# Attention with a projection woven in: a unit's value products move ahead of the dense pieces

## The chip, the cores and the metric

One NeuronCore of a Trainium2 chip runs the whole step in one launch. The metric is the device time of that core in microseconds; lower is better. Engines are named as the profile does: PE (TensorE matmul), PEld (TensorE weight load), DVE (VectorE), ACT (ScalarE), POOL (GpSimd), SP (SyncE).

## What is computed

One layer of a decoder on 1024 prompt rows and 8 sample rows: input projection, two kinds of heads, output projection, a mixture of experts, a gated embedding. The change is in the stage that computes the prompt's attention heads and, woven into them, the output projection and the router's logits. Cut to what matters there:

```
z = q @ k.T * SB_SCALE + bias                 # 8 heads of 64, strictly causal
log_beta, log_keep = log_sigmoid(z), where(mask, log_sigmoid(-z), 0)
later = cumsum(log_keep, reverse=True) - log_keep      # over the keys
a = where(mask, exp(log_beta + later), 0)
attn = a @ v
h = h + concat(attn, pool) @ w_out
m = rmsnorm(h, g_ffn)
logits = m @ [w_router_group | w_router_expert]
```

## The kernel before

The rows are cut into nine tiles of 128: tile 0 holds the 8 samples, tiles 1 to 8 the prompt. An earlier stage left qT, kT, v_sb and the pooling half of the mixed rows (mixp) in SBUF. The stage of the change begins in the trace at 296.9 us and ends at about 600 us.

**Units.** `units` lists (t, hp, g): a tile t of queries, a pair of heads hp (four of them), and a group g of up to four key blocks of 128, the last group first. Tiles 1 to 4 have one group and so four units each, with 1 to 4 key blocks; tiles 5 to 8 have two groups and eight units each. One unit n goes through these steps:

- `scores` (lines 804 to 817): PE multiplies queries by keys into `p_sc`, two heads beside each other, and adds the causal mask if the unit has the diagonal block. ACT takes two sigmoids of each head (lines 890 and 891), DVE a running product over the keys (`keep`, line 930) and the product `beta` (line 935), which are the attention weights.
- `turn` (lines 818 to 825): PE transposes `beta` into `p_at`. ACT copies it to `aT` (line 898, the semaphore `at_copied`).
- `values` (lines 826 to 837): PE waits for that copy of the same unit, `at_copied` at `turns_to["turn", n] + 1`, and multiplies it by `v_sb` into `p_o`. On the last unit of a tile, `attn` copies `p_o` to `mixT` (ACT, line 904).

The scores run three units ahead: in its turn n, PE transposes unit n, then computes the scores of unit n + 3.

**The projection.** `jobs_in` and `shares` lay the output projection of earlier tiles over the units, as pieces (j, k). k = 1 to 4 are **dense** pieces, each four matmuls of 128x128 weights by 512 columns (line 860; the trace has two records for each). k = 5 is `rows`: PE transposes the 1024 columns of h times g_ffn (line 873), ACT copies them to `hT` (line 910) and squares h (line 913). k = 6 are the router's **logits** (line 867): eight small products of `hT` by 36 columns. A tile of four units, and each half of tile 5, has the dense pieces 1 and 2 in its first unit, 3 and 4 in its second, rows in the third, logits in the fourth. Tiles 6 to 8 have one dense piece in each of their first four units, none in the fifth, rows in the sixth, logits in the seventh, none in the eighth. So 22 units are **dense units**, 8 are **rows units** and 8 are **logit units**. The tail, behind the last unit, does the ninth job by itself. DVE adds the residual to a finished half (line 949, it waits for `w_done`), multiplies it by g_ffn (line 951) and copies the logits (line 954). All jobs but the ninth share one PSUM bank, `p_w`: PE waits for `w_copied` before it fills it again.

**The order.** Every engine is a queue in program order. `plan`, `act_plan` and `dve_plan` (lines 741 to 754) are the lists that PE, ACT and DVE go through. In a unit n, ACT does: the copy of the turn; the rows; the sigmoids of unit n + 3; the attn copy. DVE does: the logits' copy; running products and beta of unit n + 3; the adds of the dense pieces. `fills` and `turns_to` are numbered from `plan`; POOL stores h and m for each `rows` in it. A stage ends in a barrier of all engines.

Of the kernel before, what the change touches and what calls it, by code (L numbers as in the profile page):

```python
# [72 lines left out]
def build(nc, A, O):  # L73
# [19 lines left out]
    with ctx:  # L93
# [635 lines left out]
        def pieces_in(n):  # L729

            of_tile = [q for q in range(len(units)) if units[q][0] == units[n][0]]
            mine = jobs_in.get(units[n][0], [])
            if not mine:
                return []
            per_job = len(of_tile) // len(mine)
            at = n - of_tile[0]
            return [(mine[at // per_job], k) for k in shares[per_job][at % per_job]]
# [3 lines left out]
        plan, act_plan, dve_plan = [[("scores", n) for n in range(3)] for _ in range(3)]  # L741
        for n in range(len(units)):
            t, hp, g = units[n]
            pieces = pieces_in(n)
            scores = [("scores", n + 3)] if n + 3 < len(units) else []
            rows = [("rows", j) for j, k in pieces if k == 5]
            dense = [("piece", (j, k)) for j, k in pieces if k < 5]
            logit = [("piece", (j, k)) for j, k in pieces if k == 6]
            end = [("values", n)] + ([("attn", t)] if n + 1 == len(units) or units[n + 1][0] != t else [])
            plan += [("turn", n)] + scores + rows + dense + logit + end  # L750
            act_plan += [("turn", n)] + rows + scores + dense + logit + end
            dve_plan += logit + scores + dense + end
        tail = [("piece", (T_ALL - 1, k)) for k in range(1, 5)] + [("rows", T_ALL - 1), ("piece", (T_ALL - 1, 6))]
        plan, act_plan, dve_plan = plan + tail, act_plan + tail, dve_plan + tail
# [1180 lines left out]
```

How the kernel before makes its waits and increments, by code:

```python
    def __call__(self, ins):  # L48
        self.n += 1
        ins.then_inc(self.sem, 1)
        self.eng.wait_ge(self.sem, self.base + self.n)
# [178 lines left out]
                def load_burst(n):  # L230
                    jj, bq = BURSTS[n]
                    if n == 0:
                        sp.wait_ge(s_const, 16 * N_CONST)
                    pages = [page_of("cache_kT", 4 * bq + g, 2 * jj + h) for g in range(4) for h in range(2)]
                    if n == 0:
                        sp.wait_ge(wlo_ready, KD)
                    else:
                        sp.wait_ge(scored, n)
                    for g in range(4):
                        for h in range(2):
                            page = pages[2 * g + h]
                            sp.dma_start(v_sb[:, 2 * g + h, :], A["cache_kT"][bass.ds(page, 1), :, :].rearrange("a p n -> (a p) n")).then_inc(s_kp, 16)
# [1 line left out]
                def load_quad(n):  # L244
                    j, bq = QUADS[n]
                    pages = [page_of("cache_v", 4 * bq + g, j) for g in range(4)]
                    if n < 2:
                        sp.wait_ge(wlo_ready, 2 * KD)
                    else:
                        sp.wait_ge(quad_done, n - 1)
                    for g in range(4):
                        page = pages[g]
                        slot = w_raw[(n % 2) * 2 + g // 2][:, (g % 2) * AW:(g % 2 + 1) * AW]
                        sp.dma_start(slot, A["cache_v"][bass.ds(page, 1), :, :].rearrange("a p n -> (a p) n")).then_inc(s_vp[n % 2], 16)
```

## Time and profile before

| | |
|---|---|
| time of the kernel, median of 3 runs | 1416.88 us (1414.88 to 1417.63) |
| the profiled execution | 1417.37 us |
| its span in the trace | 1415.5 us |
| PE busy over the span | 1301.7 us (92%) |
| DVE busy | 880.0 us (62%) |
| ACT busy | 772.2 us (55%) |
| mean granted clock of TensorE | 0.952 |

Times in rows are us from the start of the span. A row of a timeline gives start, duration, engine, line, operation, output and inputs, shapes, and how many instructions were merged (x8); in brackets stands how long the engine had stood idle before it, and for what. A granted clock of 1.00 is 2.4 GHz, 0.50 is 1.2 GHz.

### The profile page before, as it was taken

The numbers are of one execution on the slowest core, as the hardware profiler recorded it, in microseconds if no ns is written. First come the engines' busy times: TensorE is split into PE (matmuls) and PEld (weight loads), VectorE is DVE, ScalarE is ACT, GpSimd is POOL, SyncE is SP. The second block draws the span as 40 slices with busy tenths as digits, with TensorE's granted clock in tenths as the row PEclk, the third lists the DMA queues.
The fourth block names the chain that finished last, engine by engine and source line by source line (L and its number), as shares of the span: only waits on it lengthen the run. The fifth ranks groups of instructions, "written<-read, shape, count | busy, mean of one in ns | idle before, by whom it ended". The sixth has DMA issues, their size and how long they took to land. (4 is left out here: it accounts for less than half of the span.)

```text
span 1415.5 us, 18630 instructions
## 1 busy us (share of the span) xinstructions
PE 1301.7 (92%) x6716; PEld 968.1 (68%) x6716; DVE 880.0 (62%) x851; ACT 772.2 (55%) x888; POOL 214.0 (15%) x227
## 2 busy tenths in 40 slices
PE   7999899999999999717999999999999999939998
PEld 4776666755555666515788787878878788727886
DVE  5535311134535667276888888888888888735543
ACT  5435311144444656204777777777777777734452
POOL 3000100000000000023222222222222222100000
PEclk9999899979999999956999999999999999959999
DMA  8766466241112101184799999999999999631441
GB/s 303 253 238 247 165 209 225 102 172 45 45 54 80 46 3 43 50 357 166 297 369 376 374 380 378 379 380 376 377 377 381 375 372 368 255 115 70 162 153 45
DMA packets 62681, 324.29 MB, mean 229 GB/s; under 512 B 12399, under 2 KB 13839, under 8 KB 48782
## 3 DMA queue, kind: packets, MB, share of 16 engines
q1 hardware_dynamic: 44190, 272.94, 49.9%
q0 software_dynamic: 18432, 50.56, 9.7%
q8 instruction: 37, 0.61, 0.2%
q14 instruction: 22, 0.18, 0.0%
HBM read 304.96 MB, written 35.51 MB: 241 GB/s over the span
## 5 line engine op out<-in xcount | busy, mean ns | idle before, releaser
L1256 DVE TENSOR_TENSOR w_lo<-w_gate,w_hi 128x2048 fp32r<-128x2048 f32 x64 | 146.6, 2293 | 35.6 <-ACT w_hi L1252 35.6
L1256 DVE TENSOR_TENSOR w_lo<-w_down,w_hi 128x2048 fp32r<-128x2048 f32 x64 | 146.4, 2288 | 12.5 <-ACT w_hi L1252 12.5
L930 DVE TENSOR_TENSOR_SCAN keep<-keep 128x512 f32<-128x512 f32 (+3 forms) x96 | 88.5, 964 | 91.5 <-ACT beta L891 91.5
L1256 DVE TENSOR_TENSOR w_lo<-w_up,w_hi 128x2048 fp32r<-128x2048 f32 x64 | 143.6, 2286 | 0.6 <-ACT w_hi L1252 0.6
L1252 ACT ACTIVATE w_hi<-w_gate 128x2048 fp32r<-128x2048 f32 x64 | 122.2, 1913 | 28.2 <-PEq L1369 28.2
L397 PE MATMUL p_z<-w_in_hi,xT_hi 128*128 128x512 f32 (+1 forms) x288 | 119.1, 414 | 9.3 <-DVE w_in_lo L522 9.3
L1252 ACT ACTIVATE w_hi<-w_up 128x2048 fp32r<-128x2048 f32 x64 | 122.6, 1918 | 0.0
L1252 ACT ACTIVATE w_hi<-w_down 128x2048 fp32r<-128x2048 f32 x64 | 122.6, 1916 | 0.0
L398 PE MATMUL p_z<-w_in_lo,xT_hi 128*128 128x512 f32 (+1 forms) x288 | 114.2, 397 | 0.0
L399 PE MATMUL p_z<-w_in_hi,xT_lo 128*128 128x512 f32 (+1 forms) x288 | 114.1, 396 | 0.0
L1267 PE MATMUL p_y<-w_hi,hiddenT_hi 128*128 128x512 f32 x256 | 104.4, 408 | 2.1 <-DVE hiddenT_lo L1508 2.1
L1267 PE MATMUL p_g<-w_hi,xeT_hi 128*128 128x512 f32 x256 | 103.6, 405 | 2.5 <-DVE xeT_lo L1480 2.5
L1267 PE MATMUL p_u<-w_hi,xeT_hi 128*128 128x512 f32 x256 | 102.4, 400 | 0.0
L1268 PE MATMUL p_y<-w_hi,hiddenT_lo 128*128 128x512 f32 x256 | 100.9, 394 | 0.0
L1268 PE MATMUL p_g<-w_hi,xeT_lo 128*128 128x512 f32 x256 | 100.9, 394 | 0.0
L898 ACT ACTIVATE aT<-p_at 128x1024 f32<-128x1024 f32 (+3 forms) x48 | 39.6, 826 | 111.2 <-PE p_at L824 111.1
L1268 PE MATMUL p_u<-w_hi,xeT_lo 128*128 128x512 f32 x256 | 99.8, 390 | 0.0
L1359 POOL DMA_INDIRECT expert_rows<-y,idx_y x32 | 81.6, 2549 | 29.2 <-POOL idx_y L1356 29.2
L397 PEld LDWEIGHTS p_z<-w_in_hi,xT_hi 128*128 128x128 f32 (+1 forms) x288 | 51.6, 179 | 39.7 <-issue 27.3
L1273 PE MATMUL p_y<-w_lo,hiddenT_hi 128*128 128x512 f32 x256 | 69.6, 394 | 0.0
L1273 PE MATMUL p_g<-w_lo,xeT_hi 128*128 128x512 f32 x256 | 69.0, 391 | 0.1
L1273 PE MATMUL p_u<-w_lo,xeT_hi 128*128 128x512 f32 x256 | 68.4, 389 | 0.0
(271 smaller groups left out, 2552.5 us busy)
## 6 DMA issues: line engine op xcount, KB each, us to landing
w_gate<-in_w_experts SPq DMA_DIRECT2D x32, 2048.0 KB, 13.5
w_up<-in_w_experts SPq DMA_DIRECT2D x32, 2048.0 KB, 16.8
w_down<-in_w_experts SPq DMA_DIRECT2D x32, 2048.0 KB
v_sb<-in_cache_kT SPq DMA_DIRECT2D x64, 256.0 KB, 6.2
w_in_raw<-in_cache_v SPq DMA_DIRECT2D x64, 256.0 KB, 4.1
xT_raw<-in_xT_all POOLq DMA_DIRECT2D x16, 512.0 KB, 5.7
y_loaded<-expert_rows SPq DMA_DIRECT2D x8, 1024.0 KB, 7.1
x_res<-in_x_all POOLq DMA_DIRECT2D x9, 512.0 KB, 5.4
```

The lines of the kernel that those rows point to most:

```text
L397: pe.matmul(z, x_hi[par][:, k, r], w_hi[:, k, cs], start=(k == 0), stop=False)
L398: pe.matmul(z, x_hi[par][:, k, r], w_lo[:, k, cs], start=False, stop=False)
L399: ins = pe.matmul(z, x_lo[par][:, k, r], w_hi[:, k, cs], start=False, stop=(k == KD - 1))
L898: act.activation(aT[arg % 2][:].rearrange("p a b n -> p a (b n)")[:, :, 0:w], p_at[:].rearrange("p (a n) -> p a n", a=2)[:, :, 0:w], ACT.C ...
L930: ins = dve.tensor_tensor_scan(out=row, data0=row, data1=row, initial=first, op0=ALU.mult, op1=ALU.bypass)
L1252: act.activation(w_hi[slot][:], chunk_of(c, par), ACT.Copy).then_inc(hi_ready, 1)
L1256: dve.tensor_tensor(out=w_lo[slot][:], in0=chunk_of(c, par), in1=w_hi[slot][:], op=ALU.subtract).then_inc(lo_ready, 1)
L1267: pe.matmul(out, a_hi[:, k0 + k, :], w_hi[slot][:, k, :], start=(first and k == 0), stop=False)
L1268: pe.matmul(out, a_lo[:, k0 + k, :], w_hi[slot][:, k, :], start=False, stop=False)
L1273: ins = pe.matmul(out, a_hi[:, k0 + k, :], w_lo[slot][:, k, :], start=False, stop=(last and k == KC - 1))
L1359: pool.indirect_dma_start(out=y_dram, out_offset=bass.IndirectOffsetOnAxis(ap=idx_y[par][:, 0:1], axis=0), in_=y_sb[par][:], in_offset=Non ...
```

## The change

In PE's list a unit's value products (`end[:1]`) move from behind the dense pieces and the logits to directly behind the scores and the rows. The copy of a finished tile (`end[1:]`, `attn`) keeps its place, but it is no instruction of PE's. The lists of ACT and DVE, every instruction and every wait are the same; none is added or removed. Units without a piece, and rows units, have the same order as before.

```diff
             end = [("values", n)] + ([("attn", t)] if n + 1 == len(units) or units[n + 1][0] != t else [])
-            plan += [("turn", n)] + scores + rows + dense + logit + end
+            plan += [("turn", n)] + scores + rows + end[:1] + dense + logit + end[1:]
             act_plan += [("turn", n)] + rows + scores + dense + logit + end
             dve_plan += logit + scores + dense + end
```

## Rows read from the trace of the kernel before

**Rows 1.** Attention stage: stretch, length; busy PE, PEld, DVE, ACT, POOL; clock; DMA share, GB/s.
```profile
297.00:579.00 282.00, 269.95 (x1696) 162.33 (x1696) 156.07 (x186) 149.97 (x272) 13.21 (x25) 0.96 0.18 64
```

**Rows 2.** Who waited for whom in the stage: total, times, longest (us).
```profile
ACT aT L898 <- PE p_at L824: 111.1, 25, 9.3
```

**Rows 3.** SyncE timeline behind the stage: start, us, what.
```profile
605.70 0.33 SPq L1020 DMA_DIRECT2D routing_constants<-in_c_route  x1
```

**Rows 4.** A dense unit of tile 5: PE and ACT timelines (start, us, what).
```profile
408.01 1.09 PE L824 MATMUL p_at<-ident,beta 128*128 128x128 f32 x8
...
409.58 3.65 PE L860 MATMUL p_w<-w_out_sb,attn_mixed_T 128*128 128x512 f32 x8
...
416.59 1.09 PE L834 MATMUL p_o<-aT,v_sb 128*64 128x128 f32 x16
...
409.20 1.03 ACT L898 ACTIVATE aT<-p_at 128x1024 f32<-128x1024 f32 x1 [6.57 <-PE p_at L824]
```

**Rows 5.** A logit unit of tile 5, and the dense piece behind it.
```profile
421.35 1.06 PE L824 MATMUL p_at<-ident,beta 128*128 128x128 f32 x8 [0.83 <-ACT hT L910]
...
422.89 1.93 PE L867 MATMUL p_w<-w_router_sb,hT 128*128 128x36 f32 x16
425.52 1.09 PE L834 MATMUL p_o<-aT,v_sb 128*64 128x128 f32 x16 [0.71 <-ACT aT L898]
...
428.47 3.70 PE L860 MATMUL p_w<-w_out_sb,attn_mixed_T 128*128 128x512 f32 x8 [0.42 <-DVE logits L954]
...
423.85 0.70 ACT L891 ACTIVATE beta<-p_sc,per_partition 128x512 f32<-128x512 f32 x1
424.42 1.05 ACT L898 ACTIVATE aT<-p_at 128x1024 f32<-128x1024 f32 x1
```

**Rows 6.** Logit units, the first and the last of 8: logits and copy.
```profile
337.95 1.93 PE L867 MATMUL p_w<-w_router_sb,hT 128*128 128x36 f32 x16
...
339.06 0.62 ACT L898 ACTIVATE aT<-p_at 128x512 f32<-128x512 f32 x1
...
572.50 1.87 PE L867 MATMUL p_w<-w_router_sb,hT 128*128 128x36 f32 x16
...
572.76 1.02 ACT L898 ACTIVATE aT<-p_at 128x1024 f32<-128x1024 f32 x1 [0.27 <-PE p_at L824]
```

**Rows 7.** A dense unit of tile 6: its copy and its dense piece.
```profile
467.94 0.60 ACT L898 ACTIVATE aT<-p_at 128x512 f32<-128x512 f32 x1 [3.46 <-PE p_at L824]
...
468.83 3.70 PE L860 MATMUL p_w<-w_out_sb,attn_mixed_T 128*128 128x512 f32 x8
```

**Rows 8.** Dense units with a late copy, the first and the last of 13.
```profile
341.87 0.89 ACT L898 ACTIVATE aT<-p_at 128x768 f32<-128x768 f32 x1
...
342.19 3.70 PE L860 MATMUL p_w<-w_out_sb,attn_mixed_T 128*128 128x512 f32 x8
...
558.02 1.02 ACT L898 ACTIVATE aT<-p_at 128x1024 f32<-128x1024 f32 x1 [3.52 <-PE p_at L824]
...
559.04 3.65 PE L860 MATMUL p_w<-w_out_sb,pool_mixed_T 128*128 128x512 f32 x8
```

**Rows 9.** PE timeline: a dense piece and router logits at the low clock.
```profile
313.58 5.91 PE L860 MATMUL p_w<-w_out_sb,attn_mixed_T_samples 128*128 128x512 f32 x8 [0.31 <-DMA w_out_sb<-in_w_out]
...
597.26 2.97 PE L867 MATMUL p_w<-w_router_sb,hT 128*128 128x36 f32 x16 [1.20 <-ACT hT L910]
```

**Rows 10.** Groups of instructions in the stage: the products h times g_ffn.
```profile
L951 DVE TENSOR_TENSOR h_times_g<-h,g_ffn_sb 128x512 f32<-128x512 f32 x16 | 11.1, 692 | 0.5
```

**Rows 11.** Stretches around changes of TensorE's clock (columns as in Rows 1).
```profile
293.50:297.00 3.50, 2.91 (x26) 2.85 (x26) 0.03 (x1) 1.34 (x5) 0.00 (x0) 1.00 0.00 0
...
297.60:298.00 0.40, 0.40 (x5) 0.40 (x4) 0.00 (x0) 0.32 (x2) 0.40 (x2) 0.50 0.58 92
313.50:319.20 5.70, 5.62 (x8) 2.45 (x9) 2.22 (x4) 1.38 (x4) 0.00 (x0) 0.60 0.01 4
...
594.50:598.00 3.50, 1.83 (x15) 1.63 (x15) 0.41 (x1) 1.91 (x3) 0.00 (x0) 0.99 0.00 0
```

## The prediction

> **What bounds the kernel now.** I began with the share of each engine in the attention stage [rows 1]: PE is busy for 270 of 282 us, DVE for 156, ACT for 150. A busy PE is not proof of a bound, so the waits came next [rows 2]. ACT's largest wait is for PE's transposes, 111 us in 25 waits. PE's own idle time is about 12 us in the whole stage. PE sets the pace, and a wait added in PE's list is added to the stage unless a later wait of PE shrinks by as much. The next stage starts at 605.70 us, behind a barrier, and only then are expert weights asked for [rows 3]: nothing behind the stage can take up what it loses.
>
> Then I read timelines, unit by unit. In a dense unit [rows 4] PE transposes from 408.01, computes the next scores, starts the dense matmuls at 409.58 and the value products at 416.59. ACT's copy, which the values need, runs from 409.20 to 410.23. It has 6.4 us to spare: the dense pieces are its cover. In a logit unit [rows 5] PE starts the logits at 422.89. ACT is late there, since it comes from the rows unit's copy and squares and then has four sigmoids to do, the last from 423.85, before it copies from 424.42 to 425.47. PE fills part of that with 1.93 us of logits, stands for 0.71 us, and starts the values at 425.52, 0.05 us behind the copy's end.
>
> **The change, part by part.** Nothing is added or removed: the matmuls, ACT's and DVE's work and the DMAs stay. Only values move, past the dense pieces (22 units) and past the logits (8 units). SP and POOL aren't passed by anything. The direct cost is what each values product now waits for its copy, with the work that used to cover it behind it in the queue: dense pieces or logits, then the next transposes and scores, for which ACT and DVE wait.
>
> *Logit units.* The slot behind the scores is where the logits start now. Values will start at the copy's end plus 0.05, and the logits follow. Before, the end of both was the later of (slot + logits) and copy, plus values; after, it is copy plus values plus logits. The loss is the smaller of the logits' length and the copy's lateness. First of eight [rows 6]: slot 337.95, copy ends at 339.68, so 1.78 us. Tiles 3, 4 and both halves of 5 have copies 1.98 to 2.63 us late, so each loses the logits' throughput time, 1.86 (the unit of [rows 5]: 2.63 late). Tile 6 loses 1.69, tile 7 1.87, the last unit 1.33 (copy ends at 573.78, slot 572.50). Sum: 1.78 + 4 x 1.86 + 1.69 + 1.87 + 1.33 = **14.1 us**.
>
> *Dense units.* In nine of 22 the copy ends before the slot, as in [rows 7] (468.54 against 468.83), or the wait replaces one of the same length: no cost. In 13 it is late, from 0.62 us in the first to 0.05 in the last [rows 8]; the unit of [rows 4] pays 410.28 - 409.58 = 0.70. Two of the 13 stand behind a logit unit that PE leaves 1.8 us later than now, while ACT does not: their 0.62 and 0.67 go. The other eleven are 0.69, 0.70, 0.48, 0.48, 0.48, 0.20, 0.26, 0.26, 0.75, 0.05, 0.05: **4.4 us**.
>
> *Gains.* Three dense pieces wait now for DVE's copy of the logits out of `p_w`, 0.42 [rows 5], 0.42 and 0.20 us; the first waits 0.31 for w_out by DMA [rows 9]. Value products will fill these: -1.35. On the other side, h_times_g gets ready only 1.5 us behind a dense piece (an add and a product of 0.69 us each, and their starts) [rows 10], and in tile 5 the rows unit asks for it after 1.44 us, since values no longer stand between: +0.1 twice. The attn copies don't come earlier, as no dense or logit piece but the last unit's logits stands before them, and there the copy was the limit.
>
> Order alone: 14.1 + 4.4 - 1.35 + 0.2 = **17.4 us**.
>
> *TensorE's clock.* This is the cost that no row of the stage shows at the place in question, so it is bounded by its neighbours. The granted clock fell to 0.50 (1.2 GHz) at 297.6, behind small products with gaps between them (PE busy for 2.91 of 3.5 us by the record, with few columns each), and at 598.0, behind 1.83 us busy of 3.5 [rows 11], the last gap 1.20 us [rows 9]. In between it held, though PE was idle for 0.83 and 0.71 us around the logits of [rows 5]. With the change PE does 1.06 of transposes and a small score there and then stands still for some 2.5 us, where it had the logits; that is less work than before either fall. So the clock may fall in logit units: most of all in tile 4 and twice in tile 5 (2.3 to 2.6 us idle), less surely in tiles 2, 3, 6 and 7 (1.7 to 2.1), hardly in the last (1.3). A fall costs: logits 2.97 for 1.93 [rows 9, 5], +1.04; values, transposes and scores of about 2.5 us by the same ratio, +1.3; then dense pieces at the low clock until it rises. The first dense piece took 5.91 us for 3.6, and in 313.5 to 319.2 the mean clock was 0.60 [rows 11]: 4.56 us were low, half of that lost, +2.3. Together about 4.7 us a fall. Its lower bound is 1 us (it rises at once), its upper bound 8 (low through a whole logit unit, the next scores and a dense unit). From below, no falls: 0. I take three falls, in tiles 4 and 5, where the standstill is longest: 3 x 4.7 = **14.1 us**.
>
> The Trainium skill, TensorE: Matmul & The Clock Gate, section "A second HAM failure mode: psum-queue depth-cycling", says that small idle times between groups of matmuls can be enough to make the clock swing between its two levels, with the cost paid between bursts. The fall at 297.6, behind a stretch in which PE was busy for 2.91 of 3.5 us, agrees [rows 11]. By that rule every one of the seven long logit waits would be a candidate, and the sum would be that of the rival of many falls below; were the clock left out, it would be 17.4.
>
> Sum: 1417.37 + 17.4 + 14.1 = 1448.9 for the profiled execution. The median of the runs is 0.5 below that execution's time, so 1448.4, said as 1448.
>
> **Rivals.** *The clock holds, or falls once.* Each idle time is followed by a block of values at full rate. Then 17 to 22 us: about 1434 to 1439. For it: the clock held for the whole stage from 318 to 598 at the same units. Against: the new idle times are longer than any in that stretch.
> *Many falls,* five or more, since a low clock makes the next unit's small products last longer but not fuller, and at 297 to 314 such work never raised it. 17.4 + 5 x 4.7 = 41, with seven 50: 1459 to 1468. Against: dense pieces follow within a unit or two and raised it in 4.5 us.
> *Not slower.* ACT's copy is never waited for, because PE's slower pace lets ACT catch up: it has 111 us of idle time [rows 2], and in the unit behind a late one it does so. If it held everywhere, 14.1 and 4.4 vanish, and the 1.35 of gains is left: 1416. It turns on whether four sigmoids and a hT copy with squares (about 4.5 us of ACT's queue behind the rows) end before the next scores; in all eight logit units they end 1.3 to 2.6 us too late, and that chain starts at PE's rows, whatever PE's pace. A partial catch-up gives +3 to +10.
> *The edit does nothing:* units without pieces and rows units keep their order, but 30 of 48 units do change, so I give it nothing apart.
>
> **How the numbers follow.** Two to four falls (+27 to +37): 0.52. None or one: 0.17. Five or more: 0.22. Partial catch-up: 0.04. Not slower: 0.05. The likeliest gives 1448. From 1431 (clock holds, and a little of the waits is hidden) to 1465 (six falls) leaves out the top of the many falls and both catch-up cases, under 2 in 10. Within 0.2% is about 2.8 us, what a measurement can tell: same 0.03, faster 0.03, slower 0.94.
>
> **What would show it.** In the profile after: waits of PE for the aT copy at line 834 in 20-odd units, some 20 us in total; 1.7 to 2.6 us each in seven logit units; no wait for the logits' copy before dense pieces; transposes, scores and dense pieces as long as before where the clock is 1.00; a granted clock below 1.00 at some logit units of tiles 4 and 5, with logits of 2.9 us there. DVE's and ACT's busy time unchanged, the stages before and behind as long as now. It is wrong if ACT's copy in logit units ends before PE gets to the values, or if PE's added waits come back as shorter waits elsewhere.

## The result, and the profile after

The changed kernel takes 1451.69 us in the median of four runs (1448.76 to 1464.59), the kernel before 1417.26: 34.4 us slower, inside the range, 3.7 above the number forecast. The ratio on record, 1.0262 with an interval of 1.02 to 1.0325, is that of the means (37 us); the ratio of the medians is 1.0243. One run lifts the mean: it took 1464.59 us at a mean granted clock of 0.934, where the others had 0.942 to 0.944. The profiled execution is the fastest of the four, 1448.76 us.

Its page, the first line and engine totals:

```profile
span 1446.9 us, 18630 instructions
...
PE 1312.9 (91%) x6716; PEld 979.4 (68%) x6716; DVE 881.1 (61%) x851; ACT 772.7 (53%) x888; POOL 213.5 (15%) x227
```

The same instructions, and DVE and ACT as busy as before (880.0 and 772.2). PE is busy for 11 us more with the same work. The other 20 us of the span's 31.4 are idle time.

The stage alone, from its first scores to SP's first instruction behind the barrier, before and after (columns as in rows 1):

```profile
296.94:605.70 308.76, 288.05 (x1752) 172.11 (x1752) 159.06 (x191) 152.36 (x275) 14.26 (x27) 0.95 0.17 62
```

```profile
297.70:635.90 338.20, 300.20 (x1752) 184.10 (x1752) 160.33 (x191) 153.00 (x275) 14.20 (x27) 0.92 0.16 57
```

338.20 - 308.76 = 29.4 us of the 31.4 are in this stage. PE's busy time rose by 12.2 us, and its idle time (length less busy) from 20.7 to 38.0, by 17.3. So the loss seems to have two parts, waiting and a slower clock; the experiments test that. Where the idle time lies, in the waits of the changed kernel's stage:

```profile
PE p_o L834 <- ACT aT L898: 20.5, 18, 2.5
...
PE p_at L824 <- ACT hT L910: 3.4, 8, 0.8
...
PE p_at L873 <- ACT aT L898: 2.7, 4, 1.3
```

Value products wait 20.5 us for the copy; in the kernel before it was 3.4 us. The lines below it, PE's waits for the hT copy and of rows for the aT copy, are what they were in the kernel before. No wait of a dense piece for the logits' copy is left.

The dense unit of [rows 4], PE's timeline after:

```profile
417.69 1.04 PE L824 MATMUL p_at<-ident,beta 128*128 128x128 f32 x8
...
419.99 1.09 PE L834 MATMUL p_o<-aT,v_sb 128*64 128x128 f32 x16 [0.63 <-ACT aT L898]
421.02 3.70 PE L860 MATMUL p_w<-w_out_sb,attn_mixed_T 128*128 128x512 f32 x8
```

The copy that had 6.4 us to spare is now waited for 0.63 us, and the dense matmuls start behind the values.

The logit unit of [rows 5], PE and then ACT, after:

```profile
431.96 1.06 PE L824 MATMUL p_at<-ident,beta 128*128 128x128 f32 x8 [0.84 <-ACT hT L910]
...
436.13 1.98 PE L834 MATMUL p_o<-aT,v_sb 128*64 128x128 f32 x16 [2.46 <-ACT aT L898]
438.03 3.63 PE L867 MATMUL p_w<-w_router_sb,hT 128*128 128x36 f32 x16
441.47 0.67 PE L824 MATMUL p_at<-ident,beta 128*128 128x128 f32 x2
442.07 2.08 PE L811 MATMUL p_sc<-kT,qT 64*128 64x256 f32 x8
```

```profile
434.46 0.70 ACT L891 ACTIVATE beta<-p_sc,per_partition 128x512 f32<-128x512 f32 x1
435.03 1.05 ACT L898 ACTIVATE aT<-p_at 128x1024 f32<-128x1024 f32 x1
```

ACT comes to the copy 3.07 us behind the start of PE's transposes, as before (421.35 and 424.42), and PE has nothing to fill the time: 2.46 us idle instead of 0.71. Then everything is slow: values 1.98 for 1.09, logits 3.63 for 1.93, scores 2.08 for 1.13. The granted clock is low there. These are the five stretches at its low level between the first dense pieces and the tail, and two logit units in which it held (stretch, length, PE busy, clock, DMA share, GB/s):

```profile
339.50:346.30 6.80, 6.80 (x36) 0.51 0.30 101
404.40:411.20 6.80, 6.80 (x29) 0.50 0.24 89
435.10:445.30 10.20, 9.17 (x47) 0.50 0.40 130
472.60:479.40 6.80, 6.80 (x29) 0.51 0.13 51
513.60:520.40 6.80, 6.80 (x39) 0.51 0.38 119
366.80:374.40 7.60, 5.77 (x54) 1.00 0.61 208
554.70:562.20 7.50, 5.46 (x50) 1.00 0.63 210
```

The falls are in the logit units of tiles 2, 4, 5 (both) and 6; tiles 3 and 7 kept 2.4 GHz. In the kernel before there was none between tiles 2 and 8.

### The profile page after: what moved, and what is told of

Same layout as the page of the kernel before. It is cut to its first block and busy times, and to the rows that moved or that the text cites. A ratio compares the mean times of both kernels' runs of the same rounds, so it can differ in the third digit from the quotient of the medians.

```text
span 1446.9 us, 18630 instructions
## 1 busy us (share of the span) xinstructions
PE 1312.9 (91%) x6716; PEld 979.4 (68%) x6716; DVE 881.1 (61%) x851; ACT 772.7 (53%) x888; POOL 213.5 (15%) x227
```

## Experiments

All times are compared with the kernel before on the same chip: 1416.98 us in the median beside experiments 1 to 4, 1418.60 beside 5 to 8. "+x us" is worked out from the ratio on record, which is not always that of the medians; where the two differ by 0.5 us or more, both are given. For the split into waiting and clock I read the stage's windows as above.

**1. Values ahead of the dense pieces only** (the edit is against the changed kernel).

```diff
-            plan += [("turn", n)] + scores + rows + end[:1] + dense + logit + end[1:]
+            plan += [("turn", n)] + scores + rows + logit + end[:1] + dense + end[1:]
```

> Values ahead of the dense pieces, but behind the logits as before. Theory (each value product waits for its copy, and where PE stands long TensorE's clock falls): the logit units are as before, PE waits only for late copies in dense units, 4.4 us plus the 0.62 and 0.67 that the logit units no longer hide, less 1.35 of gains: +4 to +5 us on the kernel before, about 1422, and no fall of the clock between tiles 2 and 8. Rival (the whole loss comes from the dense pieces, whose length is larger and which are 22 and not 8): +20 us or more.

Measured: 1420.88 us, ratio 1.0031 (1.0013 to 1.005), +4.4 us (+3.9 by the medians). The stage:

```profile
297.32:609.32 312.00, 287.72 (x1752) 175.59 (x1752) 159.36 (x191) 152.58 (x275) 14.20 (x27) 0.95 0.17 61
```

Idle time is 24.3 us, 3.6 more than before, and busy time is the same. The mean clock stayed at 0.95, but the expectation of no fall was missed once, in the second half of tile 5:

```profile
454.60:458.00 3.40, 3.40 (x24) 2.68 (x26) 3.37 (x6) 2.30 (x6) 0.00 (x0) 0.51 0.87 269
```

```profile
454.47 1.96 PE L834 MATMUL p_o<-aT,v_sb 128*64 128x128 f32 x16 [0.50 <-ACT aT L898]
```

In that unit PE has the same list and the same wait of 0.50 us as in the kernel before, where the values took 1.09 us and the clock held. Half of 3.4 us is 1.7 us of extra busy time, and a low stretch at the beginning of the stage that is 3.4 us shorter than in the kernel before hides it. The rival, that the larger blocks cost the most, is out: 22 dense units cost an eighth of the loss.

**2. Values ahead of the logits only.** The line that takes the place of the same one:

```diff
+            plan += [("turn", n)] + scores + rows + dense + end[:1] + logit + end[1:]
```

> Values ahead of the logits, but behind the dense pieces as before. Theory: 14.1 us of waits and some five falls of the clock at 3 us: +25 to +30 us on the kernel before, 1442 to 1447. Rival (the loss is in the dense units): +5 us or less.

Measured: 1457.67 us, ratio 1.0298 (1.0271 to 1.0326), +42 us (+40.7 by the medians): more than expected, and not less than the whole change, whose interval covers this one. The stage, and three of its low stretches:

```profile
301.78:644.71 342.93, 309.35 (x1752) 186.91 (x1752) 160.05 (x191) 153.22 (x275) 14.22 (x27) 0.89 0.16 56
```

```profile
378.20:385.00 6.80, 6.80 (x30) 0.50 0.24 89
443.00:453.20 10.20, 9.89 (x45) 0.50 0.33 104
477.20:487.40 10.20, 10.04 (x46) 0.50 0.32 101
```

The idle time grew by 12.9 us (33.6 less 20.7), and with experiment 1's 3.6 that makes 16.5 of the 17.3 that the whole change adds: waits add up. The clock does not. Here it fell in the logit units of tiles 2 to 6, so in tile 3 too, and once more in the first dense piece of the tail. The unit of the second half of tile 5 was low for 10.2 us instead of 6.8, that of tile 2 for 3.4. PE's busy time is 21.3 us above the kernel before, 9.2 above the changed kernel's; of the 9.2, about 3.4 come from the low stretch at the beginning of the stage, which the edit does not touch (20.5 us here as in the kernel before, 13.6 in the changed kernel). So more low clock makes up for the 4.4 us of waits that this half lacks.

**3. The changed kernel, with PE kept at work in the logit units.** Ahead of the values stand two products of 128x128 by 512 (one in the last unit), whose result the logits overwrite:

```diff
+            fill = [("filler", (j, 1 if n + 2 == len(units) else 2)) for j, k in pieces if k == 6]
+            plan += [("turn", n)] + scores + rows + fill + end[:1] + dense + logit + end[1:]
...
+                        for _ in range(reps):
+                            pe.matmul(p_w[:], w_out[:, 0, 0:P], w_out[:, 1, 0:CHUNK], start=True, stop=True)
```

> The changed kernel, and in each logit unit two products of 128x128 by 512 (one in the last unit) into the logits' bank ahead of the values, so that PE works while it waits for the copy; their result is overwritten. Theory: waits as in the changed kernel, 17.4 us, but no fall of the clock within the stage: about +17 us on the kernel before, 1434, some 15 less than the changed kernel. Rival 1 (the clock does not matter, all is waiting): no less than the changed kernel, 1448 to 1452. Rival 2 (the clock is all of it, the waits would be absorbed): within 5 us of the kernel before.

Measured: 1435.38 us, ratio 1.0129 (1.0108 to 1.015), +18.3 us. The stage, and the logit unit of tile 4:

```profile
302.11:625.47 323.36, 299.41 (x1782) 178.74 (x1782) 160.33 (x191) 152.90 (x275) 14.21 (x27) 0.96 0.17 59
```

```profile
403.00 1.94 PE L874 MATMUL p_w<-w_out_sb 128*128 128x512 f32 x4
405.63 1.09 PE L835 MATMUL p_o<-aT,v_sb 128*64 128x128 f32 x16 [0.69 <-ACT aT L904]
406.66 1.98 PE L868 MATMUL p_w<-w_router_sb,hT 128*128 128x36 f32 x16
```

The values start as late as ever, but values and logits run at full rate, and the clock was not low between the first dense pieces and the tail. More work on PE, none of it useful, saves 16 us by the medians (34.4 less 18.4), 19 us by the ratios. In the profile the 15 filling products take some 14.5 us (1.94 for two), and with the 24.0 us of idle time that is 17.8 above the idle time of the kernel before. So the waits alone are worth some 18; both rivals are out.

**4. The changed kernel with ACT's squares behind the next unit's copy.** `h` is squared (line 913) in the logit unit, behind its turn, instead of in the rows unit:

```diff
-            act_plan += [("turn", n)] + rows + scores + dense + logit + end
+            act_plan += [("turn", n)] + [("square", j) for j, k in pieces if k == 6] + rows + scores + dense + logit + end
...
```

> The changed kernel, with ACT's squares of h (1.24 us) moved from the rows unit to behind the copy of the next unit. Theory (the copy is late because of what ACT has queued behind the rows): every logit unit's copy comes 1.1 us earlier, 8 us less of waiting than in the changed kernel, and with 0.5 to 1.5 us idle instead of 1.6 to 2.5 fewer falls of the clock, 0 to 3: 1428 to 1441. Rival (the copy's lateness follows PE's pace): as the changed kernel.

Measured: 1436.63 us, ratio 1.0141 (1.0115 to 1.0168), +20 us: 15 us less than the changed kernel by the medians, 17 by the ratios. The stage, and the logit unit of [rows 5]:

```profile
298.42:625.93 327.51, 297.55 (x1752) 181.52 (x1752) 160.59 (x191) 152.92 (x275) 14.21 (x27) 0.92 0.16 58
```

```profile
429.12 1.06 PE L824 MATMUL p_at<-ident,beta 128*128 128x128 f32 x8 [0.84 <-ACT hT L910]
...
432.25 1.98 PE L834 MATMUL p_o<-aT,v_sb 128*64 128x128 f32 x16 [1.43 <-ACT aT L898]
```

The wait is 1.43 instead of 2.46, 1.03 less; the idle time of the stage is 30.0 instead of 38.0, 8 less, as expected. So what ACT has queued behind the rows makes the copy late, and not PE's pace alone, as the rival had it. Three falls are left: here, in tile 4 (its wait 1.43 us too), and in tile 7, where PE waited only 1.01 us.

**5. The kernel before with the squares moved** (the same edit of `act_plan`).

> The kernel before with ACT's squares moved behind the next unit's copy. Theory: the copy comes 1.1 us earlier in logit units, where PE waited 0.71, 0.71, 0.50 and 0.2 us for it behind the logits, so those go: -2 us, about 1415. Rival (ACT's order does not matter with the logits as cover): no difference.

Measured: 1415.03 us, ratio 0.9975 (0.9964 to 0.9987). Faster, by 3.5 us (1.8 to 5.1 by the interval); the rival is out. The waits of the values for the copy fell from 3.4 to 2.1 us, those of dense pieces for the logits' copy from 1.0 to 0.3, together the 2 us expected.

**6. That, and values first only where the copy is early.**

```diff
+            early = t in (2, 5, 6) and any(k == 1 for j, k in pieces)
+            plan += [("turn", n)] + scores + rows + (end[:1] + dense if early else dense + logit + end[:1]) + end[1:]
```

> The kernel before with the squares moved, and values ahead of the dense pieces only in the first dense unit of tiles 2 and 6 and of both halves of tile 5, where the copy is there before the scores end and the dense piece waits for w_out or for the copy of the logits. Theory: -2 for the squares and -1.3 for the waits that the values fill, 3.3 us below the kernel before, about 1413.7. Rival: the waits come back behind the dense pieces, and it is as the kernel with the squares alone.

Measured: 1413.16 us, ratio 0.9975 (0.996 to 0.9991). By the ratio that is 3.5 us less than the kernel before, by the medians 5.4. It beats the kernel before, but is not told from experiment 5, so the value of its own part stays open. Its unit behind the logits of tile 5, where [rows 5] had a wait of 0.42 us:

```profile
423.12 1.14 PE L812 MATMUL p_sc<-kT,qT 64*128 64x256 f32 x8
424.18 0.44 PE L835 MATMUL p_o<-aT,v_sb 128*64 128x128 f32 x4
424.55 3.70 PE L861 MATMUL p_w<-w_out_sb,attn_mixed_T 128*128 128x512 f32 x8
```

PE has no gap there. But the gap to compare with is that of experiment 5:

```profile
426.69 3.70 PE L860 MATMUL p_w<-w_out_sb,attn_mixed_T 128*128 128x512 f32 x8 [0.16 <-DVE logits L956]
```

With the squares moved only 0.3 us of waits for the logits' copy were left to fill, not 1.0, and in the second half of tile 5 the values now wait 0.34 us for their own copy. Of the expectation's 1.3 us, 1.0 was for the logits' copy and was counted on the kernel before; most of that was no longer there.

**7. Experiment 2 with the filling products.**

> Values ahead of the logits only, with two filling products ahead of the values in logit units (one in the last). Theory: the 12.9 us of idle time that values ahead of the logits added stay as time (as filling or idle), and the seven falls of the clock go: +13 to +14 us on the kernel before, 1430 to 1431, and some 27 below the same order without filling. Rival (the order of the logits costs by something else than waiting and clock): over 1436.

Measured: 1431.44 us, ratio 1.0095 (1.0067 to 1.0122), +13.5 us (+12.8 by the medians), as expected, and 29 us below experiment 2 by the ratios, 28 by the medians. The clock was not low between the first dense pieces and the tail: what experiment 2 costs above its waits went with the falls.

**8. Experiment 4 with one filling product in each logit unit but the last.**

> The changed kernel with the squares moved and one filling product in the logit units (none in the last). Theory: 17.4 less 8 us of waits and no fall of the clock: +9 to +10 us on the kernel before, 1426 to 1427. Rival (waits and clock falls are not additive, each hides in the other): 1433 or more.

Measured: 1424.45 us, ratio 1.0075 (1.0044 to 1.0106), +10.6 us, but only +5.9 by the medians, and no low stretch between the first dense pieces and the tail. Three of the five runs took 1421.88 to 1424.45 us, two 1432.62 and 1435.31, at a mean clock of 0.950 instead of 0.955 to 0.959; what slowed these two is not in the one trace kept. The +9 to +10 expected lies inside the interval (+6 to +15). The rival's 1433 or more (+14) touches only the interval's upper end and is far above the median. So this fits waits and clock that add up, but does not measure it closely.

| values ahead of | as it is | squares moved | PE filled | both |
|---|---|---|---|---|
| nothing (before) | 1 | 0.9975 | | |
| dense pieces | 1.0031 | | | |
| logits | 1.0298 | | 1.0095 | |
| dense and logits (the change) | 1.0262 | 1.0141 | 1.0129 | 1.0075 |

## Why the prediction was right

**PE sets the pace, and nothing behind the stage takes the loss up.** Right: 29.4 of 31.4 us are in the stage; the next began at once behind it, as [rows 3] said.

**Waits in logit units, 14.1 us.** Right. PE's waits for the copy there were 1.62, 1.83, 2.46, 2.46, 2.25, 1.62, 2.04 and 1.17 us, where the lateness worked out from rows was 1.78, 1.98, 2.63, 2.63, 2.42, 1.69, 2.12 and 1.33. They sum to 15.45, and the kernel before had 1.92 of them behind its logits (0.71 twice and 0.50), so 13.5 were added. Experiment 7, where they stand without the clock, gave 13.5 (12.8 by the medians).

**Waits in dense units, 4.4 us less 1.35 of gains, and 0.2.** Right in the sum and nearly in each place. Of the 20.5 us of value waits, 15.5 are in logit units and 1.17 in the last unit, where it was before; 3.9 are left for dense units, and the gains of 1.35 came (no wait for the logits' copy or for w_out is left to PE's matmuls). Experiment 1, in which two more copies are late, gave 4.4 (3.9 by the medians) where 4.5 is what the sum gives. The waits for h_times_g in tile 5 came, with 0.23 and 0.22 us in place of 0.1.

**The order alone, 17.4 us.** Right. The idle time rose by 17.3, and experiment 3 gave 18.3 without falls.

**The clock, three falls at 4.7 us.** The mechanism was right and both sizes were off, in opposite directions. There were five falls, 37.4 us of low clock in all. PE's extra busy time is 12.2 us. Two things that the edit does not touch already count in it as gains: a shorter low stretch at the beginning of the stage (13.6 us for 20.5, about 3.4 us), and the tail's logits, 1.95 us instead of 2.97 [rows 9]. That makes some 16.6 us, 3.3 a fall, in the profiled execution. Experiment 3's 16 us by the medians are 3.2 a fall, its 19 us by the ratios 3.8. None is 4.7. The price failed at its term for the dense pieces, which assumed 4.56 us of low clock in them, as in the first dense piece of the stage [rows 11]. In the unit shown above the low stretch of 10.2 us was spent on values, logits and scores, and ended at 445.3, 0.6 us behind the start of the first dense matmul. The number failed at the step "where the standstill is longest": tiles 2 and 6 fell at 1.62 us, tiles 3 and 7 held at 1.83 and 2.04. That the sum still came within 4 us is luck: too few falls at too high a price, 3 x 4.7 = 14.1, for five at 3.3.

**The rivals.** That the clock falls once or never is out (five times), and that ACT catches up is out: it is late by the same 3.07 us. "Many falls", which the prediction gave 0.22 against 0.52 for two to four, came true in number, five, but not in price: 17.4 + 16.6 is 34, where its 1459 to 1468 had +41 to +50.

**The Trainium skill's rule** (TensorE: Matmul & The Clock Gate, "A second HAM failure mode: psum-queue depth-cycling") tells of another kernel, in bf16, in which small idle times between groups of matmuls made the clock swing, with the cost paid between bursts. This trace agrees so far: waits of 1.62 to 2.46 us stood before the five falls, and filling the waits took the falls away. Of the seven long logit waits, which the prediction called candidates by this rule, two had no fall.

## What to carry to other kernels

Before a consumer is moved ahead of independent work, look up when its input really lands, and on which engine's queue; the work it passes may be what covers that wait, and a short piece (here 1.9 us of logits) can be worth more than a long one. A wait on TensorE that is short and sits among small matmuls can cost as much again by the clock behind it (here some 17 and 16 us): compare busy time as well as idle time between two traces of the same work. Where a copy is late, shorten what its engine has queued ahead of it: moving 1.24 us of squares behind one copy took 3.5 us off the kernel before, which no order of PE's own list tried here is shown to do.

## What the runs showed of the hardware that was not expected

- In these traces the length of a wait does not decide alone whether the clock falls. Within the changed kernel it fell with waits of 1.62 us and held with 1.83 and 2.04; in experiment 2 the tile that had held with 1.83 fell with the same 1.83; in experiment 4 it fell with 1.01; in experiment 1 with 0.50, in a unit where the kernel before had the same list and the same 0.50 and held. What decides was not settled. Whether the falls differ in number between executions of one kernel is not shown: each kernel has one trace.
- The low stretch at the beginning of the stage differs in length: 20.5 us in the kernel before, to behind the start of the first dense piece [rows 11], but 13.6 us in the changed kernel, where it ended during the small products, 1.4 us before any instruction that the edit moves. The prediction said that such work never raised the clock. In experiment 8 it was 10.2 us. PE was at work for nearly all of it either way (columns stretch, length, PE busy, clock, DMA share, GB/s):

```profile
298.60:312.20 13.60, 13.01 (x64) 0.50 1.00 390
```

- Filling a wait with useless products of 512 columns made one kernel 16 to 19 us faster (experiment 3), and another 28 to 29 (experiment 7).
